# A hybrid block on one core: the scan's input matrices from B and the powers, each turned once and spread by SyncE's loads

## The reference

```
xr, xi = einsum('blgh,gph->blgp', u, bb_re), einsum('blgh,gph->blgp', u, bb_im)
h[t] = a * h[t - 1] + x[t]                       # complex, per group and state
y = einsum(h_re, c_re) - einsum(h_im, c_im) + d * u
y = gelu(y); y = y * sigmoid(y @ w_glu + b_glu)
```

## Time and profile before

| | |
|---|---|
| median of 3 runs | 952.34 us (951.09 to 952.35) |
| the profiled execution: its own time | 952.75 us |
| its span in the profile | 951.0 us |
| PE busy | 936.0 us |
| DVE busy | 610.0 us |
| ACT busy | 575.4 us |
| POOL busy | 111.3 us |
| weights and all else moved | 165.83 MB, mean 174 GB/s |

### The profile page before, as it was taken

The page is one execution under the profiler, slowest core; times in us unless marked ns, Lnnn a source line. Parts: engine busy times, 40 slices in busy tenths (PEclk is TensorE's granted clock), DMA queues, the critical chain, the costliest instruction groups (busy, mean ns, idle before and its releaser), DMA issues.

```text
span 951.0 us, 15769 instructions
## 1 busy us (share of the span) xinstructions
PE 936.0 (98%) x5939; PEld 796.3 (84%) x5939; DVE 610.0 (64%) x971; ACT 575.4 (60%) x928; POOL 111.3 (12%) x126
## 2 busy tenths in 40 slices
PE   7999999999999999999999999999999999999998
PEld 7998888778878999888888788888888888888886
DVE  4688889799797954855644555555555555555553
ACT  4689886876967746544545573555456545554332
POOL 3101002011020000000002540220021002200000
PEclk9999999999999999999999999999999999999999
DMA  8776544445343467555999986668999866654662
GB/s 285 185 190 196 156 133 134 136 135 175 112 140 127 137 198 266 179 192 190 175 166 180 195 239 169 182 174 160 171 160 172 197 175 178 176 175 156 212 213 85
DMA packets 116007, 165.83 MB, mean 174 GB/s; under 512 B 19301, under 2 KB 56298, under 8 KB 115690
## 3 DMA queue, kind: packets, MB, share of 16 engines
q1 hardware_dynamic: 99504, 159.67, 64.0%
q10 hardware_dynamic: 16442, 5.33, 2.3%
HBM read 162.86 MB, written 2.11 MB: 173 GB/s over the span
## 4 chain that ended last, share of the span: by engine, by line
PE 82%; ACT 7%; DVE 6%; issue 3%; DMA 1%; POOL 1%; ACTq 0%; SPq 0%; DVEq 0%
PE bank L456 21%; PE bank L458 21%; PE bank L457 21%; PE bank L483 3%; PE bank L484 3%; PE bank L485 3%; ACT wh L969 2%; ACT res L1078 2%; PE bank L600 1%; ACT res L1090 1%; DVE wl L977 1%; ACT scr L1230 1%; DVE scr L1747 1%; PE bank L592 1%; DMA res<-in_x 1%
## 5 line engine op out<-in xcount | busy, mean ns | idle before, releaser
L977 DVE TENSOR_TENSOR wl<-raw,wh 128x1024 fp32r<-128x1024 f32 x295 | 362.0, 1231 | 252.7 <-ACT wh L969 251.5
L969 ACT ACTIVATE wh<-raw 128x1024 fp32r<-128x1024 f32 x295 | 310.5, 1058 | 190.2 <-PE bank L458 119.5
L456 PE MATMUL bank<-wh,xh 128*128 128x512 f32 x768 | 307.1, 400 | 0.3 <-DVE wl L977 0.3
L458 PE MATMUL bank<-wh,xl 128*128 128x512 f32 x768 | 300.0, 391 | 0.0
L457 PE MATMUL bank<-wl,xh 128*128 128x512 f32 x768 | 299.2, 390 | 0.0
L458 PEld LDWEIGHTS bank<-wh,xl 128*128 128x128 f32 x768 | 144.1, 188 | 31.1
L456 PEld LDWEIGHTS bank<-wh,xh 128*128 128x128 f32 x768 | 144.3, 188 | 29.0 <-DVE wl L977 0.7
L457 PEld LDWEIGHTS bank<-wl,xh 128*128 128x128 f32 x768 | 144.5, 188 | 27.7
L456 PE MATMUL bank<-wh,yh 128*128 128x512 f32 x256 | 100.5, 393 | 0.0
L458 PE MATMUL bank<-wh,yl 128*128 128x512 f32 x256 | 99.7, 390 | 0.0
L457 PE MATMUL bank<-wl,yh 128*128 128x512 f32 x256 | 99.6, 389 | 0.0
(11 more groups left out here) (317 smaller groups left out, 1022.4 us busy)
## 6 DMA issues: line engine op xcount, KB each, us to landing
raw<-in_o_w_in SPq DMA_DIRECT2D x128, 512.0 KB
raw<-in_e_w_in SPq DMA_DIRECT2D x130, 256.0 KB, 3.3
raw<-in_e_w_out SPq DMA_DIRECT2D x32, 512.0 KB
raw<-in_o_w_out SPq DMA_DIRECT2D x32, 512.0 KB
raw<-in_e_w_in SPq DMA_DIRECT2D x31, 512.0 KB
raw<-in_s_w_glu SPq DMA_DIRECT2D x8, 512.0 KB
res<-in_x SPq DMA_DIRECT2D x8, 256.0 KB, 6.8
res<-in_x SPq DMA_DIRECT2D x1, 2048.0 KB, 9.6
```

The lines of the kernel that those rows point to most:

```text
L456: nc.tensor.matmul(o, l_hi, w_hi, start=first, stop=False)
L458: mm = nc.tensor.matmul(o, l_lo, w_hi, start=False, stop=last)
L969: nc.scalar.activation(wh[:, j % RING, :], raw[:, j % RING, :], ACT.Copy).then_inc(hi_done, 1)
L977: nc.vector.tensor_tensor(wl[:, j % RING, :], raw[:, j % RING, :], wh[:, j % RING, :].bitcast(F32), ALU.subtract).then_inc(lo_done, 1)
```

## The change

The scan's input matrices are no longer turned per pair. PE turns the powers once (two transposes, after slot 1 of step 0, `p_rows_turn`) and B once (eight, after slots 2 and 3, `b_rows_turn`). ACT copies the results out in slots 2 to 4 (`rows_out_of`). SP stores them to two HBM tensors, `p_rows` and `b_rows`, and loads them back for each pair in the layout of `xin`, the powers broadcast over 16 partitions (`p_load`, `b_load`). In step 0 these DMAs stand behind the loads of slots 10 to 15, in steps 1 to 3 three of them behind each of the loads of slots 6 to 9. DVE multiplies rows of B with rows of powers (`s5_rows`, two multiplies and a sum of 128 x 512 per half, slots -4 and -3), and ACT spreads the products over the two groups of `xin` (`s5_spread`, four copies of 128 x 512, slots -2 and -1).

Moved or changed beside that:
- The matrices of the scan's inputs take B times the powers 1 to 4 where it was 0 to 3, and `ca` takes C times the powers 0 to 3 where it was 1 to 4. `near` is made from B itself, copied by ACT to `b0`, and power 0 of `cc` is a copy of C by ACT (`s5_own`, four small copies in slot -6). DVE makes the powers 1 to 3 of `cc` (`s5_far`, 384 columns where it was 640, slots -7 and -5), and `s5_pad` copies 512 columns for 640.
- `mg` is made by ACT, eight copies of 128 x 64 in slot -3, where it was one instruction of DVE.
- The angles go to slots -9 and -8 (7 and 8 of the step before), the tables to slot -5.
- DVE does angles, `s5_far`, `s5_rows`, `s5_skip` behind its split of the slot's unit (`s5_ahead`), no longer ahead of it.
- `b_blocks` goes from slot 3 to slot 0 of step 0.
- The low halves of the scan's outputs are all made beside the gate chunks (`LOW_SLOT`).
- `combine` keeps p1 as it is and adds p2 times `-lam * l1 / l2` in one instruction per block; the common factor l1 drops out in the RMS norm, whose eps POOL multiplies by l1 squared (two small instructions ahead of the wait for the sums).

The core of the diff:

```diff
 
-TAB_SLOT, FAR_SLOT, BA_SLOT = [0, 0], [-7, -4], [-10, -4]
-T_SLOT = [-2, -1, -1, -1]
-NEAR_SLOT, HOLD_SLOT, SKIP_SLOT = [-1, 2], -3, -8
+TAB_SLOT, FAR_SLOT, BA_SLOT = [-9, -8], [-7, -5], [-4, -3]
+SPREAD_SLOT = [-2, -1]
+P_UNIT, B_UNIT, LOAD_UNIT = (10, 11, 12), (12, 13, 14, 15), (6, 7, 8, 9)
+NEAR_SLOT, HOLD_SLOT, SKIP_SLOT, OWN_SLOT = [-1, 2], -3, -6, -6
 X_SLOT, YN_SLOT, Y_SLOT = [0, 3], 7, [8, 8]
 IN_SLOT, OUT_SLOT = [1, 4], [5, 6]
 PAD_SLOT = [0, 4]
 GELU_SLOT, HIGH_SLOT = 9, 14
+TABLE_SLOT = -5
+LOW_SLOT = {10: 0, 11: 1, 13: 2, 15: 3}
 
...
+            def rows_aside(i, s):
+
+                if i == 0:
+                    if s == P_UNIT[0]:
+                        p_rows_keep()
+                    if s in P_UNIT[1:]:
+                        for k in range(2 * (s - P_UNIT[1]), 2 * (s - P_UNIT[1]) + 2):
+                            p_load(0, k)
+                    for k in {B_UNIT[0]: (0,), B_UNIT[1]: (1, 2, 3), B_UNIT[2]: (4, 5, 6), B_UNIT[3]: (7,)}.get(s, ()):
+                        b_rows_keep(k)
+                    if s == B_UNIT[3]:
+                        for k in range(HOP):
+                            b_load(0, k)
+                elif s in LOAD_UNIT:
+                    p_load(i, s - LOAD_UNIT[0])
+                    b_load(i, s - LOAD_UNIT[0])
 
...
+            def p_rows_turn():
+
+                pe.wait_ge(pw_done, 1)
+                for r in range(2):
+                    mm = nc.tensor.transpose(scb[:, r * P:(r + 1) * P], pw[:, r, 1:HOP + 1, :].rearrange("p k i -> p (k i)"), ident)
+                mm.then_inc(bp_ps, 1)
+
+            def b_rows_turn(half):
+
+                pe.wait_ge(bc_b, 1)
+                for b in range(2):
+                    for r in range(2):
+                        at = (2 * r + b) * P
+                        mm = nc.tensor.transpose((xb, yb)[half][:, at:at + P], bc_all[:, 2 * half + b, r, :], ident)
+                mm.then_inc(bp_ps, 1)
...
+            def s5_spread(i, r):
+
+                act.wait_ge(made_done, 2 * i + (r + 1))
+                if r == 0:
                     act.wait_ge(x_ps, 2 * i)
-                nc.scalar.activation(xin[:, 2 * k:2 * k + 2, :, :].rearrange("p i r n -> p (i r n)"), (xb, yb)[k % 2][:, :],
-                                     ACT.Copy).then_inc(xin_sb, 1)
+                    act.wait_ge(group_done, 1)
+                for g in range(2):
+                    ins = nc.scalar.activation(xin[:, :, r, 64 * g:64 * g + 64], made[r].rearrange("p (i n) -> p i n", i=TB),
+                                               ACT.Copy, scale=of_group[:, g:g + 1])
+                ins.then_inc(xin_sb, 1)
...
+            def s5_hold(i):
+
+                act.wait_ge(h_done, 2 * i) if i else act.wait_ge(prm_exp, 3)
+                for t in range(TB):
+                    ins = nc.scalar.activation(mg[:, t, :], later, ACT.Copy, scale=mag_all[:, TB * i + t:TB * i + t + 1])
+                ins.then_inc(hold_done, 1)
...
+            def s5_rows(i, r):
+
+                (pr, pi), (br, bi) = ([x[:, k, :] for k in range(2)] for x in (p_of, b_t))
+                if r == 0:
+                    dve.wait_ge(bt_in, 16 * 12 * (i + 1))
+                    first, second = prod[0].rearrange("p r n -> p (r n)"), prod[1].rearrange("p r n -> p (r n)")
+                else:
+                    first, second = pr, pi
+                v.tensor_tensor(first, pr, (br, bi)[r], ALU.mult)
+                link(v.tensor_tensor(second, pi, (bi, br)[r], ALU.mult))
+                v.tensor_tensor(made[r], first, second, ALU.add if r else ALU.subtract).then_inc(made_done, 1)
...
-                     (1, 6): b_factors, (1, 7): powers, (2, 2): lam_end, (2, 3): b_blocks}
+                     (1, 6): b_factors, (1, 7): powers, (2, 0): b_blocks, (2, 2): lam_end}
...
+                link(v.reciprocal(rec[:, k + 2:k + 4], lsum[:, k + 2:k + 4]))
+                link(v.scalar_tensor_tensor(out=rec[:, k:k + 2], in0=lsum[:, k:k + 2], scalar=nlam, in1=rec[:, k + 2:k + 4],
+                                            op0=ALU.mult, op1=ALU.mult))
                 for t, o, w in ((0, T, P), (1, 0, T)):
                     p1, p2 = s_sb[:, 2 * h, o:o + w], s_sb[:, 2 * h + 1, o:o + w]
-                    ins = v.tensor_scalar(p2, p2, rec[:, k + 2 + t:k + 3 + t], None, ALU.mult)
-                link(ins)
-                for t, o, w in ((0, T, P), (1, 0, T)):
-                    p1, p2 = s_sb[:, 2 * h, o:o + w], s_sb[:, 2 * h + 1, o:o + w]
-                    ins = v.scalar_tensor_tensor(out=p1, in0=p1, scalar=rec[:, k + t:k + t + 1], in1=p2,
-                                                 op0=ALU.mult, op1=ALU.subtract)
+                    ins = v.scalar_tensor_tensor(out=p1, in0=p2, scalar=rec[:, k + t:k + t + 1], in1=p1,
+                                                 op0=ALU.mult, op1=ALU.add)
                 ins.then_inc(p_ready, 1)
```

More of the change, by code:

```diff
@@ new lines, in p_load @@
+            def p_load(i, k):
+                sp.wait_ge(p_out, 16 * HOP)
+                if i:
+                    sp.wait_ge(xin_sb, 2 * i)
+                for g in range(2):
+                    at = slice(32 * k + 16 * g, 32 * k + 16 * g + 16)
+                    src = p_rows[k, g, :, TB * i:TB * i + TB, :].rearrange("r i n -> r (i n)")
+                    sp.dma_start(p_of[at, :, :], src.rearrange("(o r) n -> o r n", o=1).to_broadcast([16, 2, TB * 64]))\
+                        .then_inc(bt_in, 16)
@@ new lines, in b_load @@
+            def b_load(i, k):
+                sp.wait_ge(b_out, 32 * TB)
+                if i:
+                    sp.wait_ge(xin_sb, 2 * i)
+                sp.dma_start(b_t[32 * k:32 * k + 32, :, :],
+                             b_rows[:, :, :, TB * i:TB * i + TB, :].rearrange("g h f i n -> (g h) f (i n)")).then_inc(bt_in, 16)
+            def rows_aside(i, s):
[8 more added lines that the diff above has]
+                    if s == B_UNIT[3]:
+                        for k in range(HOP):
+                            b_load(0, k)
+                elif s in LOAD_UNIT:
+                    p_load(i, s - LOAD_UNIT[0])
+                    b_load(i, s - LOAD_UNIT[0])
@@ L726, in s5_out_y @@
                     mm.then_inc(y_ps, 1)
[L728 to L732 removed]
             def beside(n, s, heads):
[L735 to L738 removed]
+                s5(n, s)
                 for a, at in heads:
                     attention(a, at)
[L741 to L742 removed]
             def s5(n, s):
@@ L747, in s5 @@
                     at = s5_at(n, s, i)
-                    for k in range(2, 4):
-                        if T_SLOT[k] == at:
-                            s5_turn(i, k)
                     for h in range(2):
@@ L835, in step @@
                         beside(i, s, ([] if first else [(i - 1, s)]) + [(i, s - 2 * UNITS)])
+                        if first and s == 1:
+                            p_rows_turn()
+                        if first and 2 <= s < 4:
+                            b_rows_turn(s - 2)
                         if first and 3 <= s < UNITS - 1:
@@ L1108, in s5 @@
                     at = s5_at(n, s, i)
-                    if TAB_SLOT[1] + 1 == at:
+                    if TABLE_SLOT == at:
                         table(i)
-                    for k in range(4):
-                        if T_SLOT[k] + 1 == at:
-                            s5_turned(i, k)
+                    if OWN_SLOT == at:
+                        s5_own(i)
+                    if HOLD_SLOT == at:
+                        s5_hold(i)
+                    for r in range(2):
+                        if SPREAD_SLOT[r] == at:
+                            s5_spread(i, r)
                     for h in range(2):
@@ L1763, in s5, with s5_ahead @@
                     at = s5_at(n, s, i)
+                    for h in range(2):
+                        if IN_SLOT[h] == at:
+                            rotate_in(i, h)
+                        if OUT_SLOT[h] == at:
+                            rotate_out(i, h)
+            def s5_ahead(n, s):
+                for i in range(DA_PAIRS):
+                    at = s5_at(n, s, i)
                     for part in range(2):
@@ L1769, in s5 @@
                         if BA_SLOT[part] == at:
-                            s5_powers(i, part)
+                            s5_rows(i, part)
                     if at == SKIP_SLOT:
                         s5_skip(i)
-                    if at == HOLD_SLOT:
-                        s5_hold(i)
-                    for h in range(2):
-                        if IN_SLOT[h] == at:
-                            rotate_in(i, h)
-                        if OUT_SLOT[h] == at:
-                            rotate_out(i, h)
-                    if HIGH_SLOT + 1 == at:
-                        s5_low(i)
+                if n == DA_PAIRS and s in LOW_SLOT:
+                    s5_low(LOW_SLOT[s])
             def log_steps():
```

181 lines of the change are left out of this document (93 added, 88 removed).

## The result

The change made the kernel slower: 958.76 us (957.17 to 960.50, 5 runs) against 952.34 us, a ratio of 1.0074 with a 95% interval of 1.0062 to 1.0086. The forecast was 948.3, and its range ended at 952.6. The profiled execution took 960.12 us with a span of 958.4.

A forecast was written before the change was run, and what follows sets the result against it. PE, busy 936.0 of 951.0 us, was taken as the bound. Gains of 12.6 us (8.8 + 2.75 + 1.0) less losses of 8.6 (4.0 + 0.4 + 3.0 + 1.2) gave -4.0: 952.34 to 948.3 us, range 944.8 to 952.6.

The forecast's parts named there:

- Turns gone: Turns of the scan's input matrices leave PE: 2.2 us a pair, 8.8 us gained for four pairs.
- the three waits before the turned head output: PE's waits for DVE in slot 8, 0.29, 1.23 and 1.23 us, all go: 2.75 us gained.
- Term (1): b_blocks ahead of step 0's first split delays PE's unit to near 73.9: 4.0 us lost.
- Term (2): The other four turns of B stand in the open in slot 3 of step 0: 0.4 us lost.
- term (3): ACT late at the end of step 0; PE waits some 3 us for near copies in slot 0 of step 1.
- SP issues a DMA in about 0.46 us: Issue time used for SP's DMAs in step 0, from a median of 0.444 plus a step.
- L: SP's wait for its own stores to land, in step 0: between 2.3 and 5.6 us, taken as 4.
- that for the last loads: Landing of the loads of B's rows for pair 0: 3 us, rows there near 108.
- rival B: SP's store waits hold loads in slot 15 of step 0; 954.4 with L = 6.5; chance 0.09 whole, 0.12 part (951.5).
- Rival C: PE's clock falls to 1.2 GHz behind idle near 70.3 to 73.9: 2.3 us lost, 950.6; chance 0.07.
- Term (4): Near copies in steps 1 to 3: ACT and PE even at 26.3 us; 0.4 us a step, 1.2 lost.
- SP's extra 4 MB: SP's added DMA traffic, 4 MB against 165, taken as hidden, so no cost.

The follow-up runs named there:

- e_near_first: Changed kernel with b_blocks in slot 3, B turned after slot 5, eight B stores, plus slot 0's first-half near copies ahead of s5_pad's: 948.62 us, ratio 0.9960.
- before_b_early: The kernel before the change with only b_blocks moved from slot 3 to slot 0 of step 0: 958.97 us, ratio 1.0063.
- g_before_stores: The kernel before with 16 small SP stores behind slot 12 of step 0, three behind each of slots 6 to 9 later; profiled once, no median given.
- f_p_later: e_near_first with s5_hold as one DVE instruction and the turns of the powers after slot 2 of step 0 instead of slot 1: 946.45 us, ratio 0.9938.
- b_eight_stores: The changed kernel with B's rows stored by eight DMAs instead of sixteen: 955.15 us, ratio 1.0032.
- c_eight_fill: b_eight_stores with unread 512-column matmuls in PE's two gaps of step 0, 9 in slot 2 and 12 before the near copies: 954.94 us, ratio 1.0023.

## Why the prediction was wrong

**What held.** Turns gone and the three waits before the turned head output gone: none is left before that turn, and in e_near_first two steps win 3.9 and 3.8 us. Term (1) as a place and a size: the unit of slot 3 at 73.72, forecast 73.9; that the two agree so closely is in part luck, for in the other profiles with this edit it starts between 72.8 and 74.8 (75.2 in before_b_early). Term (2), 0.44 us. ACT's own work in term (3): 2.92 us with eight stores, forecast 3.0, and its parts measured 2.01 for `s5_hold` (forecast 2.0), 1.3 for `s5_own` (1.4) and 1.9 for `table` (1.8).

**What failed.**
- "SP issues a DMA in about 0.46 us". The median of one shape was taken for another: the new stores and loads of B's rows took 0.63 each. In g_before_stores 16 small stores, one piece to a partition, took 7.42 us, the forecast's 0.46 each, which speaks for the shape. But three weight pairs beside B's stores took 1.11 where others took 0.90 to 0.94; why is open. The guess for L, a store's landing, was too high (2.4 and 3.8 us against 4), that for the last loads too low (4.5 against 3), and the chain ended 4 us late. This is rival B's place with another cause, issue time far more than landing. It made the wait of slot 0 6.5 us instead of 3.0; eight stores gave 3.6 us of the median back, the clock's part of it included.
- Rival C had 0.07 and came true, twice: 1.2 us behind slot 3 and 2.5 behind slot 0 of step 1. I gave it little weight because no stretch inside the steps showed a gap of this size; in the later profiles the clock fell behind a wait of 1.75 us (e_near_first) and held behind one of 1.93 (f_p_later).
- The sum itself. Stalls (1) and (3) were added, but the second is the end of a chain of SP and ACT that PE's first stall only partly delays: b_blocks is worth 6.8 us alone, nothing measurable with the long chain, 2.5 with eight stores, 1.7 in the end.
- Term (4), 0.4 us a step. I compared ACT's total work with PE's time and called it even. The waits were 0.88, 0.88 and 0.76, with ACT idle 1.17 us just before the first: order, not work. Moving two copies in every step was worth 4.0 us.
- Nothing in the sum for the second layer, where 2.8 us were lost: SP's extra 4 MB were called hidden, and 1.8 us of the 2.8 are the longer wait for POOL behind the late store. Nor for the wait for the powers, 0.4 to 1.8 us in slot 1, whose own instructions were called free because they fell into another wait.

## What to carry to other kernels

When a stage is fed by a queue, write down each DMA with the issue time of its own shape, and find the chain that ends last before adding stalls: a cure of one stall shows its price only after the longer chain is cut. When work is taken off the bound engine, look at the order of small work on the feeder just ahead of the next wait, for a total that fits says nothing about it. A gap of PE can also cost what its clock loses behind it, in some runs and not in others, so look at the clock of every run.

## What the runs showed of the hardware

The granted clock fell behind gaps of 1.75 to 6.5 us, with and without turns in them, but not behind every such gap: of 12 runs of b_eight_stores three kept 1.000, one of them with gaps of 2.2 and 2.9 us. Fills of 512-column matmuls whose result nobody reads held it (1.00 in both filled stretches of c_eight_fill). A store of 16 pieces of 256 bytes from each of 16 partitions costs SP as much to issue as one of 8 pieces (0.63 us). And with 36 or 52 more small DMAs on SP's queue a much later store of ACT took 2.2 to 2.6 us longer to land. The Trainium skill (DMA: Bandwidth & Descriptors, "Queues, rings and completion order") says that each DMA engine alternates between the queues packet by packet; no run here shows which packets the store met.

The best kernel, f_p_later, by its page, part 1:

```profile
PE 931.6 (98%) x5885; PEld 792.0 (84%) x5885; DVE 593.3 (63%) x941; ACT 579.6 (61%) x947; POOL 115.4 (12%) x141
```
